# Ungained tokens into the expert gather, transposes ahead of the router logits, no scatter in the first expert pass

## The chip, the core and the metric

The kernel runs on one core of a Trainium2 chip. The metric is device time in microseconds (us), the median of the runs shown. The trace is one profiled execution of the same program. Its engines are TensorE (PE; its weight loads are PEld), VectorE (DVE), ScalarE (ACT), GpSimd (POOL) and SyncE (SP), which issues the DMAs.

## The reference

Two transformer blocks over 256 tokens of width 1024, in float32. The first has two layers with attention and gated MLPs. The second has one layer, a state-space mixer, and then the part that the change touches, a router with 16 experts in 4 groups:

```python
u2 = rmsnorm_2(h, norm_ffn[l])
h = h + hier_moe(u2, router_group_w[l], ...)
...
p_group = jax.nn.softmax((t @ wg_r + bg_r).astype(jnp.float32), axis=-1)
g_val, g_idx = lax.top_k(p_group, 1)
...
for e in range(N_EXPERTS):
    h = jax.nn.silu(t @ w_gate[e]) * (t @ w_up[e])
    out = out + combine[:, e:e + 1] * (h @ w_down[e])
```

Each token goes to one group of four experts; two of the four get a weight that is not zero. After it come a residual add and a last norm with the gain `norm_final`.

## The kernel before

**Precision.** Every large product is made of three matmuls: the weight and the activation are each split into a rounded part (high, copied by ScalarE) and a rest (low, subtracted by VectorE). A unit is 128 x 2048 weights, 1 MB. `expert_high` (ScalarE) and `expert_low` (VectorE) make the halves of unit e; TensorE waits for the semaphore `unit_low`. Eight raw buffers and four pairs of halves are in the ring.

**End of the mixer.** `hybrid_pe` ends with eight units of the output projection. In the last one every second output tile d signals `out0`, `out1`, `out2`; `hybrid_dve` then adds two tiles each time onto X (L2283, four adds, semaphore `residual`). After d = 5, and after the end, TensorE runs `to_tokens(k)`: two transposes of tile k of X (L1837), so that tokens lie on partitions, and two small matmuls with the router's weights (L1842). The mark `x_t1` stands behind the last of them. VectorE makes the low half of the first expert unit (L2408) ahead of its four adds.

**Router.** ScalarE and VectorE copy the transposed tokens into XTK (L2474, L2484, L2520) and sum their squares (L2477 to L2522); VectorE multiplies the first 512 columns by the norm's gain, GAINF, into UTF (L2518; the trace names it TMP), GpSimd the other 512 (L2610). VectorE picks each token's group by a chain of operations on a few columns (`first_max`, L2505 to L2513, run once for the groups, twice more for the experts) and its place in the group, and builds a selection matrix SEL (L2617) that also carries the token's reciprocal norm. `gather_pe` multiplies UTF by SEL (L2630, 16 fp32 products in two halves, 32 records in the trace), which puts the up to 128 tokens of a group on columns. `evacuate_act` copies each half from PSUM to UH in one operation of 512 columns (L2637), `evacuate_dve` subtracts it from PSUM into UL in one (L2645); the low half of unit 2 stands between the two on VectorE.

**Expert passes.** `one_pass(q, more)` handles the group q: for its four experts, gate units, up units, then down units, 24 units in all. A loop runs it for q = 0 to 2, and a copy of it for the last. The order within each engine is the order of the code. On TensorE: G0 and U0 (units 0 to 3), a small matmul that gathers the expert weights (L2715, waits for `comb`, the end of the router), `scatter_pe` (L2654), G1 (units 4, 5), transposes (L2684), U1 (6, 7), D0, and so on. `scatter_pe` brings the outputs of the pass before back to token order, eight matmuls of 512 columns; in pass 0 YTH, YTL and SELT are zeros (L2270 to L2272), so that it scatters nothing. VectorE: low of unit 5, `product` (L2798), `add_dve` (L2660, two adds of 1024 columns onto XTK), low of units 6 and 7. At the end of each pass but the last, the gather for the next one stands ahead of the last down product. The rest of the tokens' outputs are scattered after the last pass, and XTK is normed and written out.

## Time and profile before

| | us |
|---|---|
| median of 3 runs (1671.61 to 1672.46) | 1671.92 |
| the profiled execution's own time | 1675.16 |
| its span in the trace | 1673.4 |
| TensorE busy | 1613.5 |
| VectorE busy | 1138.2 |
| ScalarE busy | 859.2 |
| GpSimd busy | 123.4 |

The page gives each engine's busy time and its share in 40 slices of the span. A busy TensorE may still wait between two matmuls, so the waits and the timeline have to be read for what ends each wait. In the timeline, the brackets behind a row hold the idle time ahead of it and what ended it; rows that follow one another on an engine are merged, with their count. The mean granted clock of TensorE is 0.987 of full speed; 1.0 is 2.4 GHz and 0.5 is 1.2 GHz. The output projection ends near 1350 us, the router near 1377 us, and the expert passes near 1664 us.

### The profile page before, as it was taken

The page shows a single profiled execution, that of the slowest core. Times are in us where ns is not written, and L with a number is a line of the kernel's source. Part 1 is how long each engine was busy: PE and PEld are TensorE (multiplying, and loading weights), DVE is VectorE, ACT ScalarE, POOL GpSimd, SP SyncE. Part 2 cuts the span into 40 slices and gives each one's busy share as a digit, 9 for nine tenths or more (in the row PEclk, how much of TensorE's full clock was granted, in tenths as well). Part 3 has the DMA queues.
Part 4 walks back from the last instruction along what each step waited for, and adds up shares of the span by engine and source line. Part 5 has one row for each costly group of instructions (what it writes and reads, how often), then busy time and mean ns, then how long its engine had stood idle before and what let it go on. Part 6 is the DMA issues. An engine that isn't in the chain of part 4 may idle for free.

```text
span 1673.4 us, 30452 instructions
## 1 busy us (share of the span) xinstructions
PE 1613.5 (96%) x11950; PEld 1500.7 (90%) x11950; DVE 1138.2 (68%) x1391; ACT 859.2 (51%) x1040; POOL 123.4 (7%) x91
## 2 busy tenths in 40 slices
PE   6999999989999999999998999999999979999998
PEld 6999978889999999997887999989999977888886
DVE  6655676666555665557666655577767769888887
ACT  6433434664443544444456433457645346677665
POOL 1000051010000100004200100011311000000000
PEclk9999999999999999999999999999999989999999
DMA  7766641135555476674113565645533559998992
GB/s 242 239 200 183 172 151 51 27 107 196 183 190 180 151 234 195 192 181 130 60 39 101 178 199 175 185 149 178 174 115 121 187 209 327 340 350 318 362 325 112
DMA packets 236926, 309.93 MB, mean 185 GB/s; under 512 B 51156, under 2 KB 176660, under 8 KB 236836
## 3 DMA queue, kind: packets, MB, share of 16 engines
q1 hardware_dynamic: 236224, 307.61, 56.7%
q8 instruction: 55, 0.90, 0.2%
q10 hardware_dynamic: 612, 1.14, 0.2%
q14 instruction: 35, 0.29, 0.1%
HBM read 307.67 MB, written 1.05 MB: 184 GB/s over the span
## 4 chain that ended last, share of the span: by engine, by line
issue 50%; PE 38%; POOLq 3%; DVE 3%; POOL 2%; ACT 2%; DVEq 1%; DMA 1%; SPq 0%; ACTq 0%
PE psum L415 6%; PE psum L417 6%; PE psum L416 6%; PE psum L2676 3%; PE psum L2677 3%; PE psum L2678 3%; PE psum L2702 2%; PE psum L2703 2%; PE psum L2704 2%; POOL TMP L426 1%; POOLq L432 1%; PE psum L2630 1%; POOLq L1517 1%; POOL QCOS L1532 1%; DVE unit_low L407 1%
## 5 line engine op out<-in xcount | busy, mean ns | idle before, releaser
L407 DVE TENSOR_TENSOR unit_low<-unit_raw,unit_high 128x2048 fp32r<-128x2048 f32 (+1 forms) x186 | 430.6, 2316 | 223.7 <-ACT unit_high L401 223.7
L415 PE MATMUL psum<-UH,unit_high 128*128 128x256 f32 x1888 | 541.8, 287 | 16.5 <-DVE UL L465 13.1
L416 PE MATMUL psum<-UL,unit_high 128*128 128x256 f32 x1888 | 534.7, 283 | 0.0
L417 PE MATMUL psum<-UH,unit_low 128*128 128x256 f32 x1888 | 534.5, 283 | 0.0
L401 ACT ACTIVATE unit_high<-unit_raw 128x2048 fp32r<-128x2048 f32 (+1 forms) x186 | 347.8, 1871 | 119.7 <-PE psum L417 119.6
L415 PEld LDWEIGHTS psum<-UH,unit_high 128*128 128x128 f32 x1888 | 361.0, 191 | 22.6 <-DVE UL L465 15.8
L417 PEld LDWEIGHTS psum<-UH,unit_low 128*128 128x128 f32 x1888 | 361.3, 191 | 0.0
L416 PEld LDWEIGHTS psum<-UL,unit_high 128*128 128x128 f32 x1888 | 359.5, 190 | 1.6 <-issue 1.4
L2408 DVE TENSOR_TENSOR unit_low<-unit_raw,unit_high 128x2048 fp32r<-128x2048 f32 x96 | 215.5, 2287 | 30.1 <-ACT unit_high L2404 29.9
L2404 ACT ACTIVATE unit_high<-unit_raw 128x2048 fp32r<-128x2048 f32 x96 | 178.5, 1915 | 20.9 <-PE psum L417 9.1
L416 PE MATMUL psum<-HL,unit_high 128*128 128x256 f32 x640 | 179.0, 280 | 0.0
L417 PE MATMUL psum<-HH,unit_low 128*128 128x256 f32 x640 | 178.9, 280 | 0.0
L415 PE MATMUL psum<-HH,unit_high 128*128 128x256 f32 x640 | 178.3, 279 | 0.0
L415 PEld LDWEIGHTS psum<-HH,unit_high 128*128 128x128 f32 x640 | 121.4, 190 | 0.0
L416 PEld LDWEIGHTS psum<-HL,unit_high 128*128 128x128 f32 x640 | 120.2, 188 | 0.0
L417 PEld LDWEIGHTS psum<-HH,unit_low 128*128 128x128 f32 x640 | 120.2, 188 | 0.0
L555 ACT ACTIVATE SG<-SG 128x512 f32<-128x512 f32 x44 | 27.8, 632 | 153.7 <-DVE SG L596 153.6
L2676 PE MATMUL psum<-unit_high,UH 128*128 128x512 f32 x256 | 101.9, 398 | 1.5 <-DVE unit_low L2408 1.5
L2677 PE MATMUL psum<-unit_high,UL 128*128 128x512 f32 x256 | 100.9, 394 | 0.0
L2678 PE MATMUL psum<-unit_low,UH 128*128 128x512 f32 x256 | 100.7, 393 | 0.0
L559 ACT ACTIVATE HH<-H 128x512 fp32r<-128x512 f32 x40 | 25.2, 631 | 137.2 <-PE psum L417 127.0
L415 PE MATMUL psum<-UNH,unit_high 128*128 128x272 f32 (+1 forms) x320 | 93.6, 292 | 0.0
(501 smaller groups left out, 2498.3 us busy)
## 6 DMA issues: line engine op xcount, KB each, us to landing
unit_raw<-in_ffn_wg SPq DMA_DIRECT2D x44, 1024.0 KB
unit_raw<-in_ffn_wu SPq DMA_DIRECT2D x44, 1024.0 KB
unit_raw<-in_ffn_wd SPq DMA_DIRECT2D x44, 1024.0 KB
unit_raw<-in_w_in SPq DMA_DIRECT2D x36, 1024.0 KB
unit_raw<-in_expert_w_gate SPq DMA_DIRECT2D x32, 1024.0 KB, 7.4
unit_raw<-in_expert_w_up SPq DMA_DIRECT2D x32, 1024.0 KB, 8.1
unit_raw<-in_expert_w_down SPq DMA_DIRECT2D x32, 1024.0 KB, 6.7
unit_raw<-in_w_out SPq DMA_DIRECT2D x10, 1024.0 KB
```

Of the source, the lines that this page charges most:

```text
L401: act.activation(high[s][:, 0:w], raw[s][:, 0:w], ACT.Copy).then_inc(unit_high, 1)
L407: dve.tensor_tensor(low[s][:, 0:w], raw[s][:, 0:w], high[s][:, 0:w].bitcast(F32), ALU.subtract).then_inc(unit_low, 1)
L415: pe.matmul(dst, wh, xh, start=start, stop=False, skip_group_check=True)
L416: pe.matmul(dst, wh, xl, start=False, stop=False, skip_group_check=True)
L417: return pe.matmul(dst, wl, xh, start=False, stop=stop, skip_group_check=True)
L2404: act.activation(high_x[e % SPLITS][:, :], raw_x[(e + 3) % RAWS][:, :], ACT.Copy).then_inc(unit_high, 1)
L2408: dve.tensor_tensor(low_x[e % SPLITS][:, :], raw_x[(e + 3) % RAWS][:, :], high_x[e % SPLITS][:, :].bitcast(F32), ALU.subtract).then_inc(un ...
L2676: pe.matmul(psum[:, bank, :], UH[:, k, 0:P], high_x[s][:, w], start=(k == 0), stop=False)
L2677: pe.matmul(psum[:, bank, :], UL[:, k, 0:P], high_x[s][:, w], start=False, stop=False)
L2678: mm = pe.matmul(psum[:, bank, :], UH[:, k, 0:P], low_x[s][:, w], start=False, stop=(k == KT - 1))
L2702: pe.matmul(dst, hh[:, m, :], high_x[s][:, w], start=first, stop=False, skip_group_check=True)
L2703: pe.matmul(dst, hl[:, m, :], high_x[s][:, w], start=False, stop=False, skip_group_check=True)
```

## The change

Four things. The gather reads XTK, the tokens without the norm's gain. The gain is put on when the gathered tokens leave PSUM: there features lie on partitions, so that it is one value per partition, and each half is four operations of 128 columns on ScalarE and four on VectorE. GAINF, UTF, its DMA and the four multiplications, GpSimd's two among them, are gone. Second, four tiles are transposed first, then their logits are made (`turned`, `scored`), with a mark of its own for the logits. Third, the low half of expert unit 0 comes behind the first three residual adds, and on ScalarE `expert_high` of unit 1 behind the copy of the last tokens. Fourth, pass 0 is written out ahead of the loop, without `scatter_pe` and `add_dve`, and the memsets of YTH, YTL and SELT are gone.

```diff
-            def to_tokens(k):
+            def turned(k):
 
                 pe.wait_ge(residual, k // 2 + 1)
                 for n in range(2):
                     mm = pe.transpose(psum[:, 4 + 2 * n + k // 4, (k % 4) * P:(k % 4) * P + P],
                                       X[:, k, META + n * P:META + n * P + P], K[:, K_ID])
-                if k == 3:
-                    mm.then_inc(QM.sem, QM.inc("x_t0"))
+                if k % 4 == 3:
+                    mm.then_inc(QM.sem, QM.inc(f"x_t{k // 4}"))
+
+            def scored(k):
                 for n in range(2):
                     mm = pe.matmul(psum[:, 0, n * 20:n * 20 + 20], X[:, k, META + n * P:META + n * P + P], WRG[:, k, :],
                                    start=(k == 0 and n == 0), stop=(k == KT - 1), skip_group_check=True)
                 if k == KT - 1:
-                    mm.then_inc(QM.sem, QM.inc("x_t1"))
+                    mm.then_inc(QM.sem, QM.inc("logits"))
 
             for u in range(8):
                 c, r = WU + u, W_ORDER[u]
...
-                        for n in range(4):
-                            to_tokens(n)
+                        for k in range(4):
+                            turned(k)
+                        for k in range(4):
...
-            for n in range(4, KT):
-                to_tokens(n)
+            for k in range(4, KT):
+                turned(k)
+            for k in range(4, KT):
+                scored(k)
 
...
-            dve.memset(YTH[:, :].bitcast(F32), 0.0)
-            dve.memset(YTL[:, :].bitcast(F32), 0.0)
-            dve.memset(SELT[:, :].bitcast(F32), 0.0)
             dve.memset(RT[:, :, :], 0.0)
             dve.memset(PX[:, :], 0.0)
             dve.tensor_tensor(WRG[:, :, :], WR[:, :, :], GC[:, 64:72].unsqueeze(2).to_broadcast([P, KT, 20]), ALU.mult)
             w_low(dve, 7)
-            expert_low(dve, G2, 0)
             for j in range(4):
                 if j < 3:
                     dve.wait_ge(QM.sem, QM.at(f"out{j}"))
                 else:
+                    expert_low(dve, G2, 0)
                     dve.wait_ge(unit_used, used(G2, WU + 7))
                 dve.tensor_tensor(X[:, 2 * j:2 * j + 2, SEQ], two(psum[:, j, :]), X[:, 2 * j:2 * j + 2, SEQ], ALU.add).then_inc(residual, 1)
...
-            sp.dma_start(GAINF[:, :], a["norm_ffn_2_row"].to_broadcast([P, D])).then_inc(gains_in, 16)
...
-            expert_high(act, 0, G2, 1, used(G2, EU - 1))
             act.wait_ge(QM.sem, QM.at("x_t1"))
             act.activation(hh4.rearrange("p m s -> p (m s)"), psum[:, 5, :], ACT.Square, accum_out=SS[:, 0, 1:2])\
                .then_inc(BM.sem, BM.inc("ss"))
             act.wait_ge(EM.sem, EM.at("ss_sum"))
             act.activation(RS[:, 2:4], RS[:, 0:2], ACT.Sqrt, scale=1.0 / D, bias=eps[:, :]).then_inc(BM.sem, BM.inc("u_std"))
             act.activation(XTK[:, 0, 512:D], psum[:, 5, :], ACT.Copy).then_inc(BM.sem, BM.inc("xt1"))
+            expert_high(act, 0, G2, 1, used(G2, EU - 1))
             act.wait_ge(EM.sem, EM.at("g_sub"))
...
-            dve.wait_ge(gains_in, 32)
-            dve.wait_ge(BM.sem, BM.at("xt0"))
-            for n in range(2):
-                dve.tensor_tensor(UTF[:, n, 0:512], XTK[:, n, 0:512], GAINF[:, 0:512], ALU.mult)
...
-        def router_pool(pool):
-            pool.wait_ge(gains_in, 32)
-            pool.wait_ge(BM.sem, BM.at("xt1"))
-            for n in range(2):
-                ins = pool.tensor_tensor(UTF[:, n, 512:D], XTK[:, n, 512:D], GAINF[:, 512:D], ALU.mult)
-            ins.then_inc(HM.sem, HM.inc("utf"))
...
-                if half and isinstance(q, int):
-                    pe.wait_ge(HM.sem, HM.at("utf"))
                 for kk in range(4):
                     k = 4 * half + kk
                     for n in range(2):
-                        mm = pe.matmul(psum[:, GATHER_B[half], kk * P:kk * P + P], UTF[:, n, k * P:k * P + P], SEL[:, n, :],
+                        mm = pe.matmul(psum[:, GATHER_B[half], kk * P:kk * P + P], XTK[:, n, k * P:k * P + P], SEL[:, n, :],
                                        start=(kk == 0 and n == 0), stop=(n == 1), skip_group_check=True)
...
+        def ffn_gain(k):
+            return GC[:, 64 + k:65 + k]
 
         def evacuate_act(act, q):
             for half in range(2):
                 act.wait_ge(gathered, 2 * q + (half + 1))
-                act.activation(UH[:, 4 * half:4 * half + 4, 0:P], psum[:, GATHER_B[half], :].rearrange("p (k s) -> p k s", k=4),
-                               ACT.Copy).then_inc(ug_high, 1)
+                for kk in range(4):
+                    k = 4 * half + kk
+                    ins = act.activation(UH[:, k, 0:P], psum[:, GATHER_B[half], kk * P:kk * P + P], ACT.Copy, scale=ffn_gain(k))
+                ins.then_inc(ug_high, 1)
 
         def evacuate_dve(dve, q, between=lambda: None):
             for half in range(2):
                 if half:
                     between()
                 dve.wait_ge(ug_high, 2 * q + (half + 1))
-                dve.tensor_tensor(UL[:, 4 * half:4 * half + 4, 0:P], psum[:, GATHER_B[half], :].rearrange("p (k s) -> p k s", k=4),
-                                  UH[:, 4 * half:4 * half + 4, 0:P].bitcast(F32), ALU.subtract).then_inc(ug_low, 1)
+                for kk in range(4):
+                    k = 4 * half + kk
+                    ins = dve.scalar_tensor_tensor(out=UL[:, k, 0:P], in0=psum[:, GATHER_B[half], kk * P:kk * P + P], scalar=ffn_gain(k),
+                                                   in1=UH[:, k, 0:P].bitcast(F32), op0=ALU.mult, op1=ALU.subtract)
+                ins.then_inc(ug_low, 1)
 
         def scatter_pe(pe, q):
 
             for half in range(2):
-                pe.wait_ge(y_low, 2 * q + (half + 1))
+                pe.wait_ge(y_low, 2 * q + (half - 1))
                 for n in range(2):
                     for part, y in enumerate((YTH, YTL)):
                         mm = pe.matmul(psum[:, SCATTER_B[n] + half, :], SELT[:, n * P:n * P + P], y[:, half * 512:half * 512 + 512],
@@ -2656,7 +2652,7 @@
                     mm.then_inc(scattered, 1)
...
-            def one_pass(q, more):
+            def one_pass(q, more, first=False):
...
-                scatter_pe(pe, q)
+                if not first:
+                    scatter_pe(pe, q)
...
-                    if j == 1:
-                        pe.wait_ge(added, 2 * q + 2)
+                    if j == 1 and not first:
+                        pe.wait_ge(added, 2 * q)
...
-            with pe.Fori(0, last) as q:
+            one_pass(0, True, first=True)
+            with pe.Fori(1, last) as q:
                 one_pass(q, True)
             one_pass(last, False)
...
-                for n in range(2):
+                for n in range(0 if first else 2):
                     add_dve(dve, q, n).then_inc(added, 1)
```

In the order of instructions it looks so at three places. VectorE at the end of the output projection, before:

```order
L2064 SCALAR_TENSOR_TENSOR unit_low<-unit_raw,GC,unit_high 128x1024 x2
L2408 TENSOR_TENSOR unit_low<-unit_raw_118,unit_high 128x2048
L2283 TENSOR_TENSOR X<-psum,X 128x2x256 x4
L2518 TENSOR_TENSOR TMP<-XTK,GAINF 128x512 x2
L2520 COPY XTK<-psum 128x512
```

and now:

```order
L2068 SCALAR_TENSOR_TENSOR unit_low<-unit_raw,GC,unit_high 128x1024 x2
L2284 TENSOR_TENSOR X<-psum,X 128x2x256 x3
L2409 TENSOR_TENSOR unit_low<-unit_raw_117,unit_high 128x2048
L2284 TENSOR_TENSOR X<-psum,X 128x2x256
L2516 COPY XTK<-psum 128x512
```

The low half of 128x2048 has moved behind three of the four adds, and the two products with GAINF are gone.

TensorE at its last row of the output projection, where the tiles are transposed (K,X) and scored (WRG,X), before:

```order
L417 MATMUL psum<-UH,unit_low 128x256
L1837 MATMUL psum<-K,X 128x128 x2
L1842 MATMUL psum<-WRG,X 128x20 x2
L1837 MATMUL psum<-K,X 128x128 x2
...
L2455 MATMUL psum<-OH,tri_b 128x4
```

and now:

```order
L415 MATMUL psum<-UH,unit_low 128x256
L1835 MATMUL psum<-K,X 128x128 x8
L1842 MATMUL psum<-WRG,X 128x20 x8
L2455 MATMUL psum<-OH,tri_b 128x4
L2456 MATMUL psum<-OH,one_b 128x4
```

The four pairs of transposes now stand together ahead of the four pairs of logits.

VectorE at the start of pass 0 (H is the product, XTK the add, HL the low half of the transposed product), before:

```order
L2408 TENSOR_TENSOR unit_low<-unit_raw,unit_high 128x2048
L2805 REGISTER_ALU
L2806 COPY WSLOT<-psum 128x4
L2796 ISA
L2797 REGISTER_ALU
L2798 SCALAR_TENSOR_TENSOR H<-SG,WSLOT,psum 128x512
L2659 REGISTER_ALU
L2660 TENSOR_TENSOR XTK<-psum,XTK 128x1024
...
L2408 TENSOR_TENSOR unit_low<-unit_raw,unit_high 128x2048
```

and now:

```order
L2409 TENSOR_TENSOR unit_low<-unit_raw,unit_high 128x2048
L2805 COPY WSLOT<-psum 128x4
L2797 SCALAR_TENSOR_TENSOR H<-SG,WSLOT,psum 128x512
L2409 TENSOR_TENSOR unit_low<-unit_raw,unit_high 128x2048
L2409 TENSOR_TENSOR unit_low_126<-unit_raw,unit_high_125 128x2048
```

The two adds between the product and the low half of unit 6 are gone.


## Rows read from the trace of the kernel before

**Rows 1.** Waits of TensorE from 1366 us on: us in total, times, longest

```profile
PE psum L2676 <- DVE unit_low L2408: 1.5, 1, 1.5
```

**Rows 2.** Timeline, end of the output projection: start us, us, engine, line, operation [idle before <-releaser]

```profile
1345.46 1.88 DVE L2283 TENSOR_TENSOR X<-psum,X 128x512 f32<-128x512 f32 x3
1346.20 0.44 PE L1837 MATMUL psum<-K,X 128*128 128x128 f32 x2 [0.78 <-DVE X L2283]
...
1350.21 0.38 PE L1837 MATMUL psum<-K,X 128*128 128x128 f32 x2
1350.43 0.52 PE L1842 MATMUL psum<-WRG,X 128*128 128x20 f32 x4
1350.79 0.41 PE L1837 MATMUL psum<-K,X 128*128 128x128 f32 x2
1350.41 0.69 DVE L2283 TENSOR_TENSOR X<-psum,X 128x512 f32<-128x512 f32 x1 [3.07 <-PE psum L417]
...
1352.84 0.69 DVE L2520 COPY XTK<-psum 128x512 f32<-128x512 f32 x1 [0.54 <-PE psum L1842]
```

**Rows 3.** Timeline, the router's first choice on VectorE, and GpSimd beside it

```profile
1355.53 2.48 POOL L2610 TENSOR_TENSOR TMP<-XTK,GAINF 128x512 f32<-128x512 f32 x2 [87.87 <-ACT XTK L2484]
1355.87 0.94 DVE L2507 TENSOR_TENSOR RT<-RT 128x8 f32<-128x8 f32 x1
1356.89 1.15 DVE L2509 TENSOR_TENSOR RT<-RT,K 128x8 f32<-128x8 f32 x1
1358.46 0.16 DVE L2511 TENSOR_REDUCE RT<-RT 128x2 f32<-128x8 f32 x1 [0.42 <-issue]
```

**Rows 4.** Timeline, the same comparison in the router's second choice

```profile
1372.45 0.17 DVE L2507 TENSOR_TENSOR RT<-RT 128x8 f32<-128x8 f32 x1
```

**Rows 5.** Timeline, the gather and the operations that take it out of PSUM

```profile
1361.98 5.01 PE L2630 MATMUL psum<-SEL,TMP 128*128 128x128 f32 x32
1365.24 0.60 ACT L2637 ACTIVATE UH<-psum 128x512 fp32r<-128x512 f32 x1 [4.01 <-PE psum L2630]
1365.87 0.69 DVE L2645 TENSOR_TENSOR UL<-psum,UH 128x512 fp32r<-128x512 f32 x1 [0.80 <-ACT UH L2637]
```

**Rows 6.** Timeline, four ScalarE and two VectorE operations of 128 columns in a row

```profile
1279.37 1.14 ACT L1955 ACTIVATE MT<-psum,DTX 128x128 f32<-128x128 f32 x4
1360.98 0.60 DVE L2617 TENSOR_SCALAR SEL<-K,POSQ,RS 128x128 f32<-128x128 f32 x2
```

**Rows 7.** Groups by form: count, busy us, mean ns of one

```profile
L1105 ACT ACTIVATE QCOS<-QCOS,MX 128x128 f32<-128x128 f32 x52 | 20.7, 398 | 18.9 <-DVE MX L1269 18.9
```

**Rows 8.** Timeline, the first expert pass on VectorE and TensorE

```profile
1377.27 2.28 DVE L2408 TENSOR_TENSOR unit_low<-unit_raw,unit_high 128x2048 fp32r<-128x2048 f32 x1
...
1378.30 0.48 PE L2654 MATMUL psum<-YTH,SELT 128*128 128x512 f32 x1
...
1380.25 0.40 PE L2676 MATMUL psum<-unit_high,UH 128*128 128x512 f32 x1
...
1383.34 2.35 DVE L2660 TENSOR_TENSOR XTK<-psum,XTK 128x1024 f32<-128x1024 f32 x2
1385.61 4.48 DVE L2408 TENSOR_TENSOR unit_low<-unit_raw,unit_high 128x2048 fp32r<-128x2048 f32 x2
...
1387.94 0.50 PE L2676 MATMUL psum<-unit_high,UH 128*128 128x512 f32 x1 [1.52 <-DVE unit_low L2408]
```

**Rows 9.** Timeline, the boundary from pass 0 to pass 1

```profile
1433.96 3.74 PE L2630 MATMUL psum<-SEL,TMP 128*128 128x128 f32 x32
...
1440.17 6.70 DVE L2408 TENSOR_TENSOR unit_low<-unit_raw,unit_high 128x2048 fp32r<-128x2048 f32 x3 [1.11 <-ACT unit_high L2404]
...
1443.11 0.40 PE L2676 MATMUL psum<-unit_high,UH 128*128 128x512 f32 x1
```

**Rows 10.** Stretches: us, busy us of PE, PEld, DVE, ACT, POOL (instructions), PEclk, DMA share, GB/s

```profile
1353.00:1359.00 6.00, 0.00 (x0) 0.00 (x0) 4.58 (x13) 2.58 (x5) 2.48 (x2) 0.60 0.02 8
...
1362.00:1367.00 5.00, 5.00 (x34) 5.00 (x34) 3.94 (x7) 0.60 (x1) 0.00 (x0) 0.75 0.16 17
```

More of the change, by code:

```diff
@@ L324, in build @@
         RS = own("moe", "RS", [P, 4])
-        GAINF = own("moe", "GAINF", [P, D])
         GAINL = own("moe", "GAINL", [P, D])
@@ L2530, in router_dve @@
             dve.drain()
+            dve.wait_ge(QM.sem, QM.at("logits"))
             for n in range(2):
@@ L2775, in one_pass @@
                         expert_high(act, q, g, PASS_UNITS + d)
-            with act.Fori(0, last) as q:
+            one_pass(0, True, first=True)
+            with act.Fori(1, last) as q:
                 one_pass(q, True)
@@ L2845, in one_pass @@
                         expert_low(dve, g, PASS_UNITS + d)
-            with dve.Fori(0, last) as q:
+            one_pass(0, True, first=True)
+            with dve.Fori(1, last) as q:
                 one_pass(q, True)
```

24 lines of the change are left out of this document (12 added, 12 removed).

## The prediction

> **What bounds the kernel now.** I read the waits of TensorE first. From 1366 us on, where the expert passes begin, its only wait in front of a product is 1.5 us for the low half of a unit [rows 1]: the passes are bound by TensorE itself, and whatever brings it to its first fully supplied unit earlier moves the end of the run by as much. So the change can pay in two places, before the passes start and in pass 0 up to that one wait. The timelines then show what TensorE waits for there: from 1352.8 to 1362 us it does next to nothing, because a chain on VectorE runs from the copy of the last tokens (L2520, 1352.84) [rows 2] to SEL (L2617, two in 0.60 us from 1360.98) [rows 6], and on through the emptying of the gather [rows 5] and the router's second half to the low halves of units 4 to 6 [rows 8]. I follow that chain and sum what each edit does to it. Everything ahead of 1345 us is the same code and stays.
>
> **1. The last tokens come earlier: 1.8 us.** Before, VectorE makes its first residual add at 1345.46, after the low half of expert unit 0, and TensorE sits idle 0.78 us for it before the transposes at 1346.20 [rows 2]. With the three adds first, none of them waits: each becomes possible when TensorE signals its two tiles, and the first two are signalled while it works on the next. That gives 0.8. The displaced low half takes some 2.3 us (as the one of 1377.27 [rows 8]) and fits the gap of 3.07 us ahead of the fourth add [rows 2]; beside the adds that leaves about 0.8 us of cover, and if it is gone, the fourth add is late by what is missing. ScalarE's first tokens come earlier as well.
>
> The second part is the order of transposes and logits. Before, a pair of transposes starts at 1350.21, its two logits at 1350.43, the next pair at 1350.79 [rows 2]: 0.22 and 0.36 us. The mark came behind four of both, and the copy started at 1352.84. Now transposes 4 and 5 run at once, 6 and 7 wait for the fourth add, which ends at 1350.41 + 0.69 = 1351.10. Four transposes from there (0.22, and then the last pair's 0.38) bring the mark to about 1351.8: 1.0 earlier, together 1.8. The logits follow in 4 x 0.36 = 1.4 us, while VectorE needs the copy, the square sum and a reciprocal first, which hides them. Bounds: 0.8 if the logits turned out to be the later ones, 2.0 if the transposes close up fully. I take 1.8.
>
> **2. GpSimd out of VectorE's way: 2.1 us.** The comparison L2507 took 0.94 us, the product L2509 1.15, and 0.42 of idle time stood before L2511 [rows 3]. The same comparison later takes 0.17 [rows 4]; I give L2509 the same, being of the same shape. The excess is 0.77 + 0.98 + 0.42 = 2.17, less some 0.07 for the ordinary spacing: 2.1. Both slow operations end within 0.03 us of the ends of GpSimd's two multiplications with GAINF (1355.53, and 2.48 us for the two, so about 1356.8 and 1358.0) [rows 3]. These are gone. Bounds: 0, were it chance, and 2.2. I take 2.1. VectorE's own two products with GAINF stood ahead of the copy, which after them still waited 0.54 for TensorE [rows 2]; with the mark 1.8 earlier they would be in its way, but they are gone too, so they cost and give nothing, nor do the memsets, which lie in an idle stretch.
>
> **3. Emptying the gather in pieces costs 1.4 us.** One ScalarE copy of 512 columns is 0.60, one VectorE subtraction 0.69 [rows 5]. Nearest rows for the pieces: four ScalarE operations of 128 columns out of PSUM with a scale per partition, 1.14 together; two VectorE operations of 128 columns with a pointer operand 0.60, so 0.25 more for each further one and 1.1 for four [rows 6]. ScalarE +0.54 for the first half (for the second it works beside VectorE's low half of unit 2), VectorE +0.42 for each half: 1.4. Bounds: 1.1 if PSUM sources are cheaper, and 2.4 if operations don't overlap, as the 0.398 of another group [rows 7] would have it. TensorE then waits for the first half, some 0.8 us, and for the second, some 0.5; it has work to lose, since VectorE is the later one below.
>
> The Trainium skill, "VectorE: DVE Perf Modes" (the section on the TRN2 errata), speaks against such pieces: each instruction pays a fixed time, whatever its size. By its table for sources in PSUM, an estimate is +0.43 on ScalarE and +0.37 twice on VectorE, 1.2 in place of 1.4. No row here has this very form.
>
> **4. No scatter and no adds in pass 0: 2.3 us.** TensorE loses the eight matmuls from 1378.30 to 1380.25, 1.95 us [rows 8]. But at 1387.94 it had waited 1.52 for VectorE's low half of unit 6, which stood at 1385.61, behind the two adds that started at 1383.34 [rows 8]. VectorE is thus the one that counts: 1385.61 - 1383.34 = 2.27. What is late next is the low half of unit 4 (1377.27 + 2.28 = 1379.55). TensorE used to come for it at 1380.25; 1.95 earlier, it stands before it, and waits about 1.3 us there. Two units of 2.8 us each (12 matmuls by 0.23, as the eight of 1.95 show) and the transposes follow, so that TensorE comes to unit 6 within 0.1 us of VectorE. The gain is bounded by 1.5 (TensorE alone late) and 2.3.
>
> **Later passes** also have the pieces. ScalarE gets to its next high half 0.55 us later, VectorE's three low halves at 1440.17 move by that; the first of them ended 2.2 us later, at about 1442.45, and TensorE took it at 1443.11 [rows 9]. The margin of 0.65 covers 0.55. If the pieces take more, each of three boundaries pays the difference. Writing pass 0 out costs nothing: the last pass has always been a separate copy, and TensorE has no wait at its start [rows 1].
>
> **The sum.** 1.8 + 2.1 - 1.4 + 2.3 = 4.8 us. The profiled execution took 1675.16 with a span of 1673.4, so I expect a span of 1668.6 and 1670.4 for a like execution. Profiling it cost 3.2 over the median; against the median of 1671.92 the forecast is **1667.1**.
>
> **Rivals.**
>
> *The clock never falls, or rises sooner.* TensorE was granted 0.60 in the quiet 6 us and 0.75 in the stretch of the gather [rows 10]; its 32 matmuls took 5.01 us, against 3.74 at the later boundary [rows 5, 9]. The first half would then be ready 1.3 us sooner, and VectorE, idle 0.80 before and 0.5 more by step 3, can use all of it: 1665.8. For: the quiet shrinks by 3.9 us. Against: 0.60 over 6 us is 1.2 us at the high level and 4.8 at the low one, so it fell some 1.4 us after the last logits, and more than 5 us of quiet remain. The Trainium skill, "TensorE: Matmul & The Clock Gate" ("What's actually happening"), has the clock follow how busy the array has lately been; that leaves both open. Chance 0.09.
>
> *Pieces without overlap.* ScalarE 4 x 0.40 = 1.6 and VectorE 4 x 0.34 = 1.4: 1.0 + 0.7 + 0.7 = 2.4 in step 3, and at the boundaries 1.1 - 0.65 = 0.4, three times. 1667.1 + 1.0 + 1.2 = 1669.3. For: [rows 7]. Against: those write an accumulator between, and [rows 6] have no such thing. Chance 0.12.
>
> *The slow comparisons have another cause* and stay: 1667.1 + 2.1 = 1669.2. Only the two matching ends speak against it, but twice. Chance 0.08.
>
> *Slower: the clock stays low into the projections.* Each unit of 2.8 us costs 2.8 more at 1.2 GHz, the waits of steps 3 and 4 (0.5 + 1.3) swallow 1.8, and the gain is 4.8. From 6.6 / 2.8 = 2.4 units at the low clock the change loses; with all four units of G0 and U0, 11.2 - 6.6 = 4.6 slower, 1676.5. For: the array now waits between the gather and unit 0, between 0 and 1, and before 4. Against: each of these is shorter than the 1.4 us that it took the clock to fall before, and work stands between them. Chance 0.05.
>
> *The gain of the early mark is not passed on* and small prices add up, to half the sum: 1669.5. Chance 0.06.
>
> **How the numbers follow.** The forecast has 0.60, with 1666.0 to 1668.3 for its own bounds. A measurement of this kernel can tell about 0.2%, 3.3 us, from no change, which is 1668.6. Faster: 0.60 + 0.09, and 0.02 of the next cases, 0.71. Within: the rest of the three cases near 1669.3, 0.24. Slower: 0.05. The range reaches from the clock's case to the two of pieces and comparisons: 1665.5 to 1669.4.
>
> **What would show it.** L2507 and L2509 at 0.17 each with GpSimd silent; the copy of the last tokens some 1.8 us earlier and SEL 3.9; no TensorE wait of 0.78 at the transposes. Four small operations per half, 1.1 us on either engine. In pass 0 TensorE waits before unit 4 for about 1.3 us and hardly before unit 6, where 1.52 stood. From there to the end every stretch is as long as before. It would be wrong if TensorE waited at the start of passes 1 to 3, if the comparisons stayed slow, or if the granted clock were below 1.0 after unit 0.

## The result, and the profile after

The changed kernel has a median of 1665.62 us over 14 runs (1660.89 to 1671.44), the kernel before 1671.85 beside it (14 runs, 1668.0 to 1672.86). The ratio is 0.9968, with a 95% interval from 0.9958 to 0.9979: 6.2 us faster (3.5 to 7.0 by the interval), where 4.8 were forecast. A second measurement (below) gave 4.6. The profiled execution has a span of 1659.1 us, 14.3 less than that of before; it took 1660.89, the fastest of its 14, while that of before, with 1675.16, is slower than all 14 beside it. Two thirds of those 14.3 us are not the change, as the next rows show. They are VectorE's timeline (start us, us of the row, what runs, and in brackets the idle time ahead and what ended it) in the last projection of the state-space mixer, in code that is the same in both kernels: before, then after.

```profile
1326.34 2.48 DVE L2064 SCALAR_TENSOR_TENSOR unit_low<-unit_raw,GC,unit_high 128x1024 fp32r<-128x1024 f32 x2 [2.42 <-ACT unit_high L2055]
```

```profile
1316.68 2.48 DVE L2068 SCALAR_TENSOR_TENSOR unit_low<-unit_raw,GC,unit_high 128x1024 fp32r<-128x1024 f32 x2 [2.42 <-ACT unit_high L2059]
```

The same operation, behind the same idle 2.42 us, comes 9.7 us earlier. From here on I count from this row, the anchor, and call what follows it the tail: 1673.36 - 1326.34 = 347.0 us before, 1659.08 - 1316.68 = 342.4 after. The tail is **4.6 us** shorter; the sum of the prediction was 4.8.

The timeline of the changed kernel where the first two steps act, VectorE and TensorE:

```profile
1333.03 0.69 DVE L2284 TENSOR_TENSOR X<-psum,X 128x512 f32<-128x512 f32 x1 [7.91 <-PE psum L415]
...
1335.63 1.03 PE L1835 MATMUL psum<-K,X 128*128 128x128 f32 x8
1336.44 2.28 DVE L2409 TENSOR_TENSOR unit_low<-unit_raw,unit_high 128x2048 fp32r<-128x2048 f32 x1
...
1339.92 0.69 DVE L2284 TENSOR_TENSOR X<-psum,X 128x512 f32<-128x512 f32 x1 [1.21 <-PE psum L415]
1340.67 0.66 PE L1835 MATMUL psum<-K,X 128*128 128x128 f32 x4 [0.35 <-DVE X L2284]
1341.37 0.69 DVE L2516 COPY XTK<-psum 128x512 f32<-128x512 f32 x1 [0.75 <-PE psum L1835]
...
1344.40 0.17 DVE L2507 TENSOR_TENSOR RT<-RT 128x8 f32<-128x8 f32 x1
1344.65 0.17 DVE L2509 TENSOR_TENSOR RT<-RT,K 128x8 f32<-128x8 f32 x1
...
1347.68 0.60 DVE L2607 TENSOR_SCALAR SEL<-K,POSQ,RS 128x128 f32<-128x128 f32 x2
```

The first transposes start with no idle time ahead, where 0.78 us stood [rows 2]; the low half of unit 0 has moved into the gap ahead of the fourth add, which is 1.21 us instead of 3.07. Both router operations that took 0.94 and 1.15 us [rows 3] take 0.17. And the gather, its pieces, and pass 0:

```profile
1348.67 4.78 PE L2618 MATMUL psum<-SEL,XTK 128*128 128x128 f32 x32
...
1351.70 1.14 ACT L2630 ACTIVATE UH<-psum,GC 128x128 fp32r<-128x128 f32 x4 [2.66 <-PE psum L2618]
1352.87 1.13 DVE L2640 SCALAR_TENSOR_TENSOR UL<-psum,GC,UH 128x128 fp32r<-128x128 f32 x4 [1.12 <-ACT UH L2630]
1354.05 0.50 PE L2672 MATMUL psum<-unit_high,UH 128*128 128x512 f32 x1 [0.60 <-DVE UL L2640]
...
1357.29 0.50 PE L2672 MATMUL psum<-unit_high,UH 128*128 128x512 f32 x1 [0.19 <-DVE UL L2640]
...
1364.92 2.28 DVE L2409 TENSOR_TENSOR unit_low<-unit_raw,unit_high 128x2048 fp32r<-128x2048 f32 x1
...
1367.35 0.47 PE L2672 MATMUL psum<-unit_high,UH 128*128 128x512 f32 x1 [1.12 <-DVE unit_low L2409]
...
1373.35 0.48 PE L2672 MATMUL psum<-unit_high,UH 128*128 128x512 f32 x1
```

Four pieces take 1.14 us on ScalarE and 1.13 on VectorE. TensorE now waits before units 0, 1 and 4, and no longer before unit 6, where 1.52 us stood [rows 8]. Its list of waits over the whole span (us in total, times, longest) has the same three for a product of the passes, and none at the later passes:

```profile
PE psum L2672 <- DVE unit_low L2409: 1.1, 1, 1.1
...
PE psum L2672 <- DVE UL L2640: 0.8, 2, 0.6
```

Counted in the distances between these rows and those of [rows 2, 6, 8], with unit 0 of the kernel before:

```profile
1366.74 0.48 PE L2676 MATMUL psum<-unit_high,UH 128*128 128x512 f32 x1
```

| stretch | before | after | difference |
|---|---|---|---|
| anchor to the copy of the last tokens | 26.50 | 24.69 | -1.81 |
| copy to SEL | 8.14 | 6.31 | -1.83 |
| SEL to unit 0 | 5.76 | 6.37 | +0.61 |
| unit 0 until TensorE comes for unit 4 (before: for the scatter) | 11.56 | 12.18 | +0.62 |
| from there to unit 6 | 9.64 | 7.12 | -2.52 |
| unit 6 to the end | 285.42 | 285.73 | +0.31 |

### The profile page after: what moved, and what is told of

It is laid out like the page before. It is cut to its first block, busy times and chain, and to the rows that moved or that the text cites. A ratio compares the mean times of both kernels' runs of the same rounds, so it can differ in the third digit from the quotient of the medians.

```text
span 1659.1 us, 30391 instructions
## 1 busy us (share of the span) xinstructions
PE 1602.8 (97%) x11942; PEld 1490.3 (90%) x11942; DVE 1134.0 (68%) x1408; ACT 861.0 (52%) x1062; POOL 121.0 (7%) x89
## 3 DMA queue, kind: packets, MB, share of 16 engines
q10 hardware_dynamic: 612, 1.14, 0.2%
## 4 chain that ended last, share of the span: by engine, by line
issue 49%; PE 39%; POOLq 3%; DVE 3%; POOL 2%; ACT 1%; DVEq 1%; DMA 1%; SPq 0%; ACTq 0%
PE psum L413 6%; PE psum L415 6%; PE psum L414 6%; PE psum L2672 3%; PE psum L2673 3%; PE psum L2674 3%; PE psum L2698 2%; PE psum L2699 2%; PE psum L2700 2%; POOL TMP L424 1%; POOLq L430 1%; POOLq L1515 1%; PE psum L2618 1%; POOL QCOS L1530 1%; DVE unit_low L405 1%
```

## The experiments

Single executions of one and the same kernel lie up to 10 us apart, so each run is read twice: by its median against the kernel before on the same chip, and by the tail of its profiled execution. The 95% interval of a ratio reaches about 0.001 to either side, which is 1.4 to 2.4 us, so that medians alone can't tell parts of 1 us. The gather inside the tail varies by itself, from 3.8 to 6.3 us, with the clock that TensorE is granted there; the last column takes it out.

| run | median, minus before's | tail | gather | tail without gather |
|---|---|---|---|---|
| before | | 347.0 | 5.01 | 342.0 |
| after | -6.2 | 342.4 | 4.78 | 337.6 |
| again | -4.6 | 343.2 | 6.32 | 336.9 |
| b_gain | -0.9 | 346.7 | 5.11 | 341.6 |
| b_order | -2.5 | 345.3 | 4.81 | 340.5 |
| b_peel | -1.8 | 345.8 | 6.05 | 339.8 |
| c_pool | -4.2 | 345.0 | 6.25 | 338.8 |
| c_scatter | -2.9 | 344.8 | 5.11 | 339.7 |
| c_whole | -6.6 | 341.8 | 5.54 | 336.3 |
| c_warm | -7.6 | 341.5 | 3.81 | 337.7 |

With the tail's code as it was before, the last column is the same each time: two kernels further down that change nothing behind the anchor have gathers of 5.85 and 6.28 us, and 342.0 too. The changed kernel has 337.6 with a gather of 4.78, 337.7 with 3.81 and 336.9 with 6.32. Behind the slow gather TensorE has no wait before unit 0, where 0.60 us stood, because the pieces of the first half are done by then; there the column takes out 0.7 us too much. A row without brackets had no idle time ahead of it (the second execution of the changed kernel, run again):

```profile
1354.40 6.32 PE L2618 MATMUL psum<-SEL,XTK 128*128 128x128 f32 x32
...
1360.54 0.50 PE L2672 MATMUL psum<-unit_high,UH 128*128 128x512 f32 x1
```

So the change is worth 4.4 us with a gather of about 5 us and 5.1 with one of 6.3, the gather's own time aside.

### The changed kernel once more

> The changed kernel once more, for its spread and for a second trace. The theory (T: the chain on VectorE from the last tokens to the low half of unit 6 sets when the expert passes begin, 4.8 us shorter) expects 1665 to 1669 us and, from the end of the output projection to the start of unit 6, the same time as in the first trace of the changed kernel, to 0.5 us, but for the gather, where the granted clock decides. Rival (R: TensorE's clock in the unchanged part is what differs between the two profiled executions): the end of the output projection lies anywhere between 1330 and 1342 us in this trace, with other stretches at the low clock ahead of it.

Measured: 1666.96 us against 1671.6, ratio 0.9978 (0.9967 to 0.9989). The two measurements of the same pair, 6.2 and 4.6 us, enclose the forecast. The anchor comes at 1322.44 us in this trace, 5.8 us later than in the first trace of the same kernel, so that time ahead of the anchor differs without any change. From the anchor to SEL it is 30.97 us, and 31.00 in the first trace.

### One part alone, on the kernel before

Only the gain moved:

```diff
-                ins = pool.tensor_tensor(UTF[:, n, 512:D], XTK[:, n, 512:D], GAINF[:, 512:D], ALU.mult)
...
-                act.activation(UH[:, 4 * half:4 * half + 4, 0:P], psum[:, GATHER_B[half], :].rearrange("p (k s) -> p k s", k=4),
-                               ACT.Copy).then_inc(ug_high, 1)
+                for kk in range(4):
+                    k = 4 * half + kk
+                    ins = act.activation(UH[:, k, 0:P], psum[:, GATHER_B[half], kk * P:kk * P + P], ACT.Copy, scale=ffn_gain(k))
```

> The kernel before with only the gain moved: the gather reads the tokens without it, GpSimd's and VectorE's products with the gain row are gone, each half leaves PSUM in four operations of 128 columns. T expects the two slow comparisons of the router at 0.17 us each (2.1 gained) and 1.4 lost in the gather's emptying: -0.7 us in all, 1671.2. A rival that puts the slow comparisons down to something other than GpSimd expects them unchanged and +1.4 us.

Only the order (transposes ahead of logits, three residual adds ahead of the low half of unit 0):

```diff
-                        for n in range(4):
-                            to_tokens(n)
+                        for k in range(4):
+                            turned(k)
+                        for k in range(4):
+                            scored(k)
...
-            expert_low(dve, G2, 0)
```

> The kernel before with only the order changed: transposes ahead of logits, the three residual adds ahead of the low half of expert unit 0, ScalarE's high half of unit 1 behind the last tokens. T expects the copy of the last tokens 1.8 us earlier after the last matmul of the seventh output tile, and since VectorE's two products with the gain row now stand between (1.3 us, and they wait for the first tokens, which come earlier), up to 0.7 of it lost again: -1.1 to -1.8 us, 1670.1 to 1670.8. A rival by which the logits are the later ones expects -0.8.

Only pass 0 written out, without scatter and additions:

```diff
-            with pe.Fori(0, last) as q:
+            one_pass(0, True, first=True)
+            with pe.Fori(1, last) as q:
```

> The kernel before with only pass 0 written out without scatter and adds. T expects TensorE to wait about 1.3 us before unit 4 and hardly before unit 6, the wait of 1.52 gone, and 2.2 us gained: 1669.7. Rival: only TensorE's own 1.95 us count and the wait at unit 6 stays, or the written-out pass costs fetches, with waits of TensorE without a releaser at its start and at the start of pass 1.

Measured: ratios 0.9995 (0.9986 to 1.0004), 0.9989 (0.9981 to 0.9998) and 0.999 (0.9982 to 0.9999). The three differences of the medians add up to -5.1 us, and the whole change gave -4.6 on the same chip; the gain alone can't be told from no change by its median. The tails without the gather are closer: 0.4, 1.5 and 2.3 us for the parts, 4.2 together, and 4.4 for the whole. The parts are nearly independent. In the trace with the gain moved alone both router operations are at 0.17 us, and the pieces take 1.13 and 1.12 with TensorE waits of 0.71 and 0.17 before units 0 and 1: what GpSimd's absence gives, the pieces take back to all but 0.4 us. With the order alone the copy comes only 1.5 us nearer to the anchor, since VectorE's two products with GAINF still stand ahead of it, and the TensorE wait before unit 6 is 1.50. In the third, TensorE's only wait of pass 0 is before unit 4:

```profile
1376.88 0.47 PE L2673 MATMUL psum<-unit_high,UH 128*128 128x512 f32 x1 [1.21 <-DVE unit_low L2405]
```

### GpSimd put back beside the router

```diff
+        def router_pool(pool):
+            pool.wait_ge(gains_in, 16)
+            pool.wait_ge(BM.sem, BM.at("xt1"))
+            for n in range(2):
+                ins = pool.tensor_tensor(OTOK[:, n, 512:D], GAINL[:, 0:512], GAINL[:, 512:D], ALU.mult)
```

> The changed kernel, with GpSimd's two products put back at the place in time where they ran before: after the last tokens' final addition it multiplies two halves of the gain tile, two operations of 512 elements per partition, into a buffer that nobody reads afterwards. TensorE, VectorE and ScalarE keep the changed kernel's order. Theory (GpSimd stood in VectorE's way): the router's short comparisons, 0.17 us each in the changed kernel, fall back to about 0.9 to 1.2 us as in [rows 3], and where they meet the two products the chain from the last addition to the gathered tokens gets 1 to 2.1 us longer, so the median comes out 0.5 to 2.1 us above the changed kernel's. Rival (the comparisons were slow for another reason, by their place behind the residual addition or the gain products of VectorE): they stay at 0.17 us and the time stays within 0.3 us.

Timeline of that kernel, GpSimd and VectorE:

```profile
1345.89 2.48 POOL L2607 TENSOR_TENSOR TMP<-GAINL 128x512 f32<-128x512 f32 x2 [82.77 <-ACT XTK L2483]
...
1345.99 0.16 DVE L2505 TENSOR_REDUCE RT<-RT 128x2 f32<-128x8 f32 x1
1346.23 0.94 DVE L2507 TENSOR_TENSOR RT<-RT 128x8 f32<-128x8 f32 x1
1347.25 1.15 DVE L2509 TENSOR_TENSOR RT<-RT,K 128x8 f32<-128x8 f32 x1
1348.47 0.16 DVE L2511 TENSOR_REDUCE RT<-RT 128x2 f32<-128x8 f32 x1
1348.71 0.17 DVE L2513 TENSOR_TENSOR RT<-RT 128x8 f32<-128x8 f32 x1
```

The two durations of [rows 3] are back to the hundredth, 0.94 and 1.15, with nothing changed but two multiplications on GpSimd whose result nobody uses. Each slow operation ends where a multiplication of GpSimd ends (half of 2.48 behind 1345.89 is 1347.13, the end 1348.37; the operations end at 1347.17 and 1348.40). From the copy to SEL it takes 8.07 us, against 6.31 without: 1.8, not 2.1. The idle 0.42 us ahead of L2511 [rows 3] did not come back, so that this part was not GpSimd's. The tail is 1.8 us longer than in run again, whose gather was as slow (6.25 and 6.32). By the medians the price is 0.5 to 2 us. This is shown, and the rival that the operations are slow for another reason has fallen. The Trainium skill, "SBUF — State Buffer" (the section "Who interferes with whom"), says that a VectorE instruction with two inputs in SBUF contends with a GpSimd instruction that reads SBUF, and that the ports the two engines share are an exclusive lock, where the order of issue decides who blocks. By that rule, the trace agrees: L2507 and L2509 have two inputs, start behind a multiplication and wait for its end. The reduction L2505 has one input, and beside the first multiplication it took 0.16 us (1345.99 to 1346.15), as L2511 did behind the second.

### Pass 0 written out, but with its scatter

```diff
-                if not first:
-                    scatter_pe(pe, q)
+                scatter_pe(pe, q)
...
-                for n in range(0 if first else 2):
+                for n in range(2):
```

> The changed kernel, with its first expert pass still written out ahead of the loop, but with that pass's scatter matmuls, their additions into the sums and the zeroing of the sums put back. Theory (what pays is the scatter and the additions left out): VectorE has its two additions of about 2.35 us each back between the low halves, TensorE waits about 1.5 us before unit 6 as in [rows 8], and the median is about 2 us above the changed kernel's. Rival (what pays is that the pass is written out, so that its instructions are not those of the loop): the median stays within 0.3 us of the changed kernel's and no wait before unit 6 comes back.

```profile
1381.89 2.35 DVE L2659 TENSOR_TENSOR XTK<-psum,XTK 128x1024 f32<-128x1024 f32 x2
1384.16 4.49 DVE L2412 TENSOR_TENSOR unit_low<-unit_raw,unit_high 128x2048 fp32r<-128x2048 f32 x2
```

The two additions stand ahead of the low halves of units 6 and 7 again, and TensorE's wait before unit 6 is back, with 1.17 us. The tail without the gather is 2.1 us longer than that of the changed kernel (339.7 and 337.6, with the same waits before units 0 and 1), the median 1.8 (-2.9 against the -4.6 of the second measurement, on another chip). What is left out pays. That writing the pass out is neither gain nor loss is seen to a few tenths: 2.3 us come with the pass alone, and 2.1 go with the scatter.

### Each half emptied by one operation

The norm gain of the gathered tokens is left out of this kernel's computation.

```diff
-                for kk in range(4):
-                    k = 4 * half + kk
-                    ins = act.activation(UH[:, k, 0:P], psum[:, GATHER_B[half], kk * P:kk * P + P], ACT.Copy, scale=ffn_gain(k))
-                ins.then_inc(ug_high, 1)
+                act.activation(UH[:, 4 * half:4 * half + 4, 0:P], psum[:, GATHER_B[half], :].rearrange("p (k s) -> p k s", k=4),
+                               ACT.Copy).then_inc(ug_high, 1)
```

> The changed kernel, with each half of the gathered tokens of a pass emptied from PSUM by one operation of 512 elements on ScalarE and one on VectorE in place of four with a pointer each; the norm gain of the gathered tokens is left out of the computation for that. Theory (the pieces lengthen the chain): the ScalarE copy goes from 1.14 to about 0.60 us and the VectorE one from 1.13 to about 0.70 us, TensorE's waits before units 0 and 1 of the first pass (0.60 and 0.19 us) shrink by 0.7 to 0.9 us in all, and the start of unit 0 is 0.8 to 1.4 us nearer to the last low half of the projections; the median is 0.6 to 1.4 us below the changed kernel's. Rival (the pieces overlap with the gather matmuls and cost nothing): the start of unit 0 and the median stay within 0.3 us.

```profile
1355.75 0.60 ACT L2628 ACTIVATE UH<-psum 128x512 fp32r<-128x512 f32 x1 [1.19 <-PE psum L2618]
...
1357.40 0.68 DVE L2636 TENSOR_TENSOR UL<-psum,UH 128x512 fp32r<-128x512 f32 x1
```

No TensorE wait before units 0 and 1. Without the gather the tail is 336.3 us, 1.3 less than in the changed kernel's first execution (337.6, gather 4.78), close to the 1.4 of step 3, and 0.6 less than in its second (336.9, gather 6.32), where the slow gather covers the first half. The median is 1665.05, below both of the changed kernel's, but by less than the intervals can tell. The pieces are the price of the moved gain.

### TensorE kept busy in the router

Fill-in matmuls into a free PSUM bank, 8 ahead of the counts and 6 ahead of the positions:

```diff
+        def filler(pe, n):
+            for i in range(n):
+                pe.matmul(psum[:, 1, 0:P], K[:, K_ONE], K[:, K_ID], start=True, stop=True, skip_group_check=True)
```

> The changed kernel, with fill-in matmuls of 128 columns into an unused PSUM bank in TensorE's two waits of the router, 8 ahead of the counts and 6 ahead of the positions; their results are not used. Theory (the gather is slow because TensorE's clock has fallen to 1.2 GHz in the router's idle stretch): the granted clock stays at 1.00 there, or rises sooner, the first gather half of 32 matmuls takes about 3.7 us as in [rows 9] in place of 4.78, and the start of unit 0 is 0.7 to 1.3 us earlier, the median likewise. Rival (the fill-in matmuls delay the router's own ones by more than they give back, or the clock falls all the same): the gather stays near 4.8 us, and the median is 0 to 1.5 us above the changed kernel's.

The 32 records of the gather that the expectation names are the whole of it, not a half. First the two stretches of the changed kernel (us, busy us of PE, PEld, DVE, ACT and POOL with their instructions, granted clock, DMA share, GB/s), then the same part with the fill-in matmuls, and its gather:

```profile
1342.00:1348.00 6.00, 1.69 (x16) 1.50 (x16) 4.27 (x27) 4.88 (x7) 0.00 (x0) 0.66 0.20 82
1348.00:1355.00 7.00, 6.40 (x40) 5.99 (x40) 5.47 (x14) 3.69 (x10) 0.00 (x0) 0.81 0.26 78
```

```profile
1351.00:1358.00 7.00, 5.98 (x55) 5.60 (x54) 4.94 (x27) 5.56 (x8) 0.00 (x0) 1.00 0.31 128
...
1358.64 3.81 PE L2624 MATMUL psum<-SEL,XTK 128*128 128x128 f32 x32 [0.33 <-DVE POSQ L2615]
```

With 6 of 7 us busy in place of 1.7 of 6, the clock stays at its full 2.4 GHz, and the gather takes 3.81 us, near the 3.74 of the later boundary [rows 9]. The tail is 0.9 us shorter than the changed kernel's in one execution and 1.7 shorter than in the other. The median, 1664.09, is the lowest of the study (ratio to before 0.9953, 0.9938 to 0.9967); but its interval overlaps with the changed kernel's, so that it beats the kernel before clearly and the changed one by the trace alone.

### Where the 9.7 us ahead of the change come from

The last four runs asked whether the rest of the spread is the same effect. In these stretches of the layers (between two residual additions), the granted clock of one and the same code differs between executions. Attention of the first layer: after, before, and with the router's fill-in matmuls, which are not near it:

```profile
201.91:361.51 159.60, 151.88 (x1190) 130.53 (x1189) 109.02 (x275) 82.96 (x195) 31.09 (x20) 1.00 0.30 91
```

```profile
201.82:362.98 161.16, 153.44 (x1190) 132.08 (x1189) 109.05 (x275) 82.95 (x195) 31.10 (x20) 0.99 0.30 90
```

```profile
202.17:364.85 162.68, 154.97 (x1190) 133.60 (x1189) 109.04 (x275) 82.99 (x195) 31.12 (x20) 0.98 0.29 89
```

At mean clocks of 1.00, 0.99 and 0.98 the same 1190 matmuls take 159.6, 161.2 and 162.7 us. All 14 traces fall on these three: 159.5 to 159.6 in five, 161.1 to 161.3 in eight, 162.7 in one. TensorE's matmuls of a gated MLP follow a wait of 2.4 to 2.6 us, so I filled those waits:

```diff
+            pe.wait_ge(consts_in, 32)
+            for n in range(10):
+                pe.matmul(psum[:, 7, 0:P], K[:, K_ONE], K[:, K_ID], start=True, stop=True, skip_group_check=True)
             projection(G_BANK, g, c0, True)
```

> The kernel before, unchanged from its state-space mixer on, with ten fill-in matmuls of 128 columns, results unused, in TensorE's queue ahead of each of the four gated MLPs of the two layers, where it waits 2.4 to 4.5 us for VectorE. Theory (the spread between executions of one kernel, and the 9.7 us by which the two profiled executions differ ahead of the changed code, are stretches of low TensorE clock that follow these waits and differ between executions): the low-clock stretches near 370, 563 and 918 us of the profiled execution are gone, the median comes out 3 to 5 us below the kernel before, and the time of single executions spreads less. Rival (the clock falls there whatever TensorE does, or falls for the layer's attention waits alone): the stretches stay and the median is within 1 us of the kernel before, or above it by the fill-in work that outlasts a wait, 0.5 us or less each.

Measured: 1677.14 us, 5.9 slower than before (ratio 1.0036, 1.0022 to 1.005), although the trace has no low clock at all ahead of the router. The fill-in work reads the constants, and at the start of the program these are not there yet:

```profile
19.25 4.40 PE L544 MATMUL psum<-K 128*128 128x128 f32 x20 [7.35 <-DMA K<-in_constants]
23.41 0.36 PE L415 MATMUL psum<-UH,unit_high 128*128 128x256 f32 x1
```

The first MLP begins at 23.4 us; it began at 16.1. That was my mistake. It is not the whole loss: the stretch of the second layer's first MLP takes 192.84 us here without any low clock, and 190.46 in the changed kernel, also without any. There the fill-in matmuls did not fill the wait but ran behind an idle stretch of 2.26 us, and the first product starts 8.7 us behind the residual addition in place of 6.3:

```profile
566.39 2.47 PE L544 MATMUL psum<-K 128*128 128x128 f32 x20 [2.26 <-issue]
568.62 0.36 PE L415 MATMUL psum<-UH,unit_high 128*128 128x256 f32 x1
```

Both also hold for the next kernel, the changed one with both sorts of fill-in matmuls and the copy of the positions behind the low half of unit 4:

> The changed kernel with three additions: the fill-in matmuls in the router's two waits of TensorE (8 and 6), the ten fill-in matmuls ahead of each gated MLP, and VectorE's copy of the token positions (0.42 us) placed behind the low half of unit 4. If both effects of the clock are real and add up: about 1.4 us below the changed kernel for the router, 3 to 5 us for the MLPs, 0.3 us for the copy (TensorE's wait of 1.12 us before unit 4 becomes 0.8), together 1661 to 1664 us, 8 to 11 us below the kernel before. If the fill-in work ahead of the MLPs gives nothing: 1664 to 1666 us, as with the router's fill-in matmuls alone.

Measured: 1672.21 us (ratio 1.0009, 1.0 to 1.0018), for the same reasons. The copy's part came as expected: TensorE's wait before unit 4 is 0.79 us in place of 1.12. The two were made again with fill-in matmuls ahead of the second MLP of each layer alone:

```diff
+                for n in range(10):
+                    pe.matmul(psum[:, 7, 0:P], K[:, K_ONE], K[:, K_ID], start=True, stop=True, skip_group_check=True)
                 mlp_pe(pe, 2 * l + 1, 3 * l + 2, g, C3)
```

> The kernel before with ten fill-in matmuls of 128 columns ahead of the second gated MLP of each layer alone, where TensorE waits 2.57 us in the profiled execution; the constants that they read are in place by then, so that they can't hold up the start of the kernel as they did in the run with all four MLPs (first unit of the first MLP at 23.4 in place of 16.1 us). If the clock theory holds, the low-clock stretches near 370 and 918 us are gone (each 3.4 us at half speed, so 1.7 us each) and the median is 2 to 3.5 us below the kernel before. If the fill-in work is itself on the path or the clock falls for another cause: within 0.5 us of the kernel before or above it.

> The changed kernel with the router's fill-in matmuls, the fill-in matmuls ahead of the second MLP of each layer, and the copy of the positions behind the low half of unit 4 (TensorE's wait there 0.79 us, as in the run before this one, in place of 1.12). If the effects add up: 1.5 + 2 to 3.5 + 0.3 us below the changed kernel, 1660 to 1663 us, 8.5 to 11 us below the kernel before, and a narrower spread of single executions than the changed kernel's 10.5 us. If the MLPs' part gives nothing: 1664 to 1665 us.

Measured: 1673.25 us, 2.0 slower than before (ratio 1.0012, 1.0003 to 1.0021), and 1665.98 (0.997, 0.9959 to 0.9981), no better than the changed kernel. The stretch that holds the filled wait, and the one behind it, before and then with the fill-in matmuls:

```profile
362.98:555.77 192.79, 188.03 (x1572) 186.98 (x1571) 112.90 (x90) 82.23 (x68) 7.92 (x3) 0.99 0.55 177
555.77:748.09 192.32, 189.40 (x1590) 188.89 (x1589) 114.31 (x99) 88.26 (x73) 4.99 (x3) 0.99 0.65 191
```

```profile
363.14:555.88 192.74, 189.06 (x1592) 187.76 (x1591) 112.84 (x90) 82.23 (x68) 7.92 (x3) 1.00 0.54 176
555.88:750.56 194.68, 190.46 (x1590) 189.95 (x1589) 114.27 (x100) 88.24 (x73) 4.96 (x3) 0.98 0.64 189
```

My theory fell in half. In the second MLP the clock is now at 1.00, and the stretch is as long as before (192.74 for 192.79): low clock cost nothing there. TensorE does not set the length of that stretch: at the full clock it waits for VectorE after every few of its first products, where at the low clock it came late enough not to wait. One of these waits, with the fill-in matmuls:

```profile
369.19 0.39 PE L415 MATMUL psum<-UH,unit_high 128*128 128x256 f32 x1 [0.41 <-DVE UL L465]
```

In the first MLP of the next layer, where nothing was changed, the clock is lower than before and the stretch 2.4 us longer (in the changed kernel's profiled execution it took 190.46 at 1.00). So the clock explains the 9.7 us: 1.6 of them in the first attention, 1.9 in that MLP, 3.1 in the second attention and 3.3 in the state-space mixer, by the same distances. What decides in which of them it falls is not settled. In these two kernels, filling one wait did not buy it away: the next stretch had more of the low clock. The Trainium skill, "TensorE: Matmul & The Clock Gate" ("What's actually happening"), says that the gate is not tied to a kernel's start, and puts the penalty of its ramp below 1% of a typical kernel's span. By that, the trace agrees: the changed kernel's fastest and slowest executions, with mean clocks of 0.993 and 0.988, took 1660.89 and 1671.44 us, 0.6% apart. The mean clock alone does not give the time, since another one with 0.988 took 1667.74.

## Why the prediction was right

**Step 1, last tokens earlier.** Forecast 1.8, in the trace 1.81, of it 0.83 up to the fourth add (forecast 0.8) and 0.98 from there to the copy (forecast 1.0). No wait at the first transposes; the marks of the last four came as worked out, with a wait of 0.35 for the fourth add. With the order changed alone it is 1.5, because VectorE's products with GAINF stood in the way. The prediction had said so, and priced them at nothing only because the same change removes them.

**Step 2, GpSimd out of the way.** Forecast 2.1, in the trace 1.83 and, put back, 1.76 (8.07 to 6.31). The mechanism was right and the term 0.3 too large. The two slow operations are as forecast; the 0.42 of idle time was counted to GpSimd without a sign for it. From L2507 to L2511 it was 1358.46 - 1355.87 = 2.59 us [rows 3] and is 0.49. But from L2511 to SEL it now takes 2.79 us, where it took 2.52 (1360.98 - 1358.46 [rows 3, 6]). Of the 0.27 that came back, 0.18 is in one row, as idle time of the same sort ("issue"). With GpSimd put back this row stays and the 0.42 does not return, so that GpSimd's own share is 1.75. Why the idle time moves is open.

```profile
1345.79 0.17 DVE L2536 TENSOR_TENSOR RT<-RT,K 128x8 f32<-128x8 f32 x1 [0.18 <-issue]
```

**Step 3, the pieces.** Forecast 1.4. Measured +0.61 to unit 0 and +0.62 behind it, 1.2 together, with a gather that was 0.23 faster, so 1.4 to 1.5. Against whole operations it is 1.3, and 0.6 behind a slow gather. ScalarE took 1.14 for four pieces, as the nearest row had it [rows 6], VectorE 1.13: 0.54 more than one operation, and 0.44 more for each half, 1.4 together. The estimate from the Trainium skill, "VectorE: DVE Perf Modes" (the section on the TRN2 errata), was 0.43 and twice 0.37, 1.2 together, and this trace does not agree with it. TensorE's waits were 0.60 and 0.19 against forecast 0.8 and 0.5; a wait counts more from start to start than as idle time: the one of 0.19 widened the distance between its two matmuls from 0.23 to 0.58. The rival of pieces without overlap (2.4) has fallen.

**Step 4, no scatter in pass 0.** Forecast 2.3, measured 2.52 from the scatter's place to unit 6, 2.3 with this part alone and 2.1 when it was put back. TensorE waits 1.12 before unit 4 (forecast 1.3), and not at all before unit 6. The chain on VectorE had set the gain, not TensorE's eight matmuls.

**Later passes.** The three low halves begin 6.75 us after the gather in place of 6.21 [rows 9]: 0.54, forecast 0.55, and the margin of 0.65 held, for TensorE waits nowhere at a boundary. From unit 6 to the end it took 0.31 us longer all the same, where nothing was forecast: 0.15 up to the next gather, 0.06 in the two passes between gathers, 0.10 behind the last. No wait shows why, and I leave it open.

**The clock.** It fell again, as the likeliest case had it: a granted clock of 0.66 in the quiet, 0.81 in the gather. That the quiet shrank did not help for sure: the gather took 4.78 and 6.32 us, and 5.01 to 6.28 in the four traces with the router of before. Nowhere did it stay low into the projections, so the slower case did not come. But the argument against that case was weak: the clock did not need 1.4 us to fall, it fell 0.9 and 0.6 us behind the last logits in the two executions (logits to 1343.03 and 1348.76, low clock from 1343.9 and 1349.4), and yet it stayed up through the wait of 1.12 us before unit 4.

**The sum.** 4.8 forecast; 4.6 by the tail, 6.2 and 4.6 by medians. That it fits so well is in part luck: the steps gave 1.81 + 1.83 - 1.23 + 2.52, and 0.31 was lost behind them, so that errors of 0.2 to 0.3 either way cancelled. What the prediction did not have is the size of the chance differences ahead of the change. It took "everything ahead of 1345 us is the same code and stays" for a statement on time; that it is the same code is right, and its time differed by 9.7 us between the two profiled executions. The expected span of 1668.6 was missed by 9.5 for this reason alone, while the median came within 1.5.

## What to carry to other kernels

Measure a small change from a row that both kernels share, just ahead of it: here the tails without the gather gave 4.4 and 5.1 us from single executions, when the spans differed by 14.3 and 7.7, and the medians of the same pair by 6.2 and 4.6. Look for short two-input VectorE operations whose ends coincide with those of GpSimd's: an engine that is hardly busy (7%) cost 1.8 us by standing beside them. And before leaving work out of the engine that is the bound, read which engine the next wait is for: TensorE's eight matmuls were 1.95 us, VectorE's adds 2.27, and it was the second that came back, to 0.3 us.

## What the runs showed of the hardware that was not expected

- An operation of 8 columns on VectorE, 0.17 us by itself, took 0.94 and 1.15 us beside a GpSimd multiplication of 512 columns, to the hundredth the same in two kernels: it ended when the other did. A reduction of 8 columns with one input kept its 0.16 us beside it.
- The same 32 gather matmuls took 3.81 us with the clock kept up and up to 6.32 us behind a quiet stretch.
- The granted clock of unchanged code differs between executions at six or seven places of this kernel, and each cost from nothing (the second MLP: 192.74 and 192.79 us) to 3.3 us (the state-space mixer).
- Raising the mean granted clock is no gain by itself: the kernel with four filled waits had 0.996, the highest of all profiled executions, and its median was 5.9 us above that of the kernel before.
